# DSA outputs scaled by transposed reciprocals, scores of a job in neighbouring PSUM banks, one bank for outputs

## The chip, the cores and the metric

The kernel runs on one core of a Trainium2 chip. The metric is the device time of one execution in microseconds. Engines are named as in the profile: PE (TensorE; PEld is its weight load), DVE (VectorE), ACT (ScalarE), POOL (GpSimd), SP (SyncE, which issues the DMAs).

## The reference

One layer of a decoder on 1024 tokens with 16 meta tokens in front, width 1024, all float32. The input is RMS-normalised and projected; two attentions of 8 heads of 64 channels run side by side, stick-breaking attention (SB) and sparse attention chosen by an indexer (DSA). Their outputs are gated, merged, projected and followed by a squared-ReLU MLP. The part that the change touches is DSA for a block of 128 queries:

```python
logits = jnp.einsum('bqhd,bqkhd->bhqk', qb, kg) * (D_HEAD ** -0.5)   # kg: the 256 selected keys
logits = jnp.where(sel_ok[:, None], logits, -jnp.inf)
p = jax.nn.softmax(logits, axis=-1)
return jnp.einsum('bhqk,bqkhd->bqhd', p, vg)
```

The kernel does not gather: it computes all causal scores and adds a mask (`sel`, 0 or -1e30) for the keys that are not selected. The softmax divides by the row sum of the exponents.

## The kernel before, in words

Matrix products are made of float32 parts rounded to the PE's format: x = hi + lo, and a product is hi*hi + hi*lo + lo*hi, three matmuls. A stage of projections comes first (line 606), then 64 SB jobs, between which the rest of the projections is filled in, then 64 DSA jobs, then the branch stage (o_hi and o_lo times the branch weights, gates), the output projection and the MLP.

A job is one head and one block of 128 queries; block i has KEYS[i] = 16 + 128(i+1) keys, 144 to 1040. Each head takes its blocks in the order 7, 0, 6, 1, 5, 2, 4, 3 (`BLOCKS`). `JOBS` has the 64 SB jobs and then the 64 DSA jobs; NJ = 128. Every engine runs the same loop over j and does in iteration j, in this order:

- PE: `scores(j)` (line 637: keys in chunks of at most 512 columns, even in size, two matmuls each, into PSUM banks 2 and 3 in turn); `turn(j-2)` (657: transposes the weights a_buf, up to four 128-key tiles in one bank, a "group", into a ring of banks 4, 5, 6 and in the DSA stage also 0); the next head's `values` when j % 8 = 4; `product(j-3)` (667: three matmuls a tile into the output bank, 7 or 1 in turn in the DSA stage).
- DVE: in the DSA stage the reciprocal of job j-1's sum (`normalise`, 1028); `logits(j)` (1010: one instruction a chunk adds the mask to the score and takes the running minimum of the negated sum; each is recorded as two instructions on line 1024); `rest_weights(j-2)` (1038: the lo part of the transposed weights, which also frees the bank); for the last 16 jobs `rest_output` (1052: the lo part of an output).
- ACT: `normalise(j-1)` (781, line 785: a_buf times the reciprocal, in place); `round_weights(j-2)` (786: the hi part); `exponent(j)` (773, line 778: exp with the row sum as by-product); `output(j-3)` (805: copies a product out of PSUM, to `o_pair` for the first 48 DSA jobs, and for the last 16, `PAIRED` and later, as hi part straight to `o_hi`). `round_pair` (821) casts a finished pair of heads (16 jobs) of `o_pair` to `o_hi` in iterations `PAIR_AT`; POOL takes the rest.
- SP: loads queries, keys and values of the next head (`load_head`) when the last scores of the head before are done.

An instruction waits for semaphores (`wait_ge`) that others count up; `turn_bank` (620) waits for the bank's last group to be freed, `product` for the last output of its bank. The queue of an engine is in order.

Of the kernel before, what the change touches and what calls it, by code (L numbers as in the profile page):

```python
# [20 lines left out]
P = 128  # L21
# [84 lines left out]
NZ_SB = Z_END[NJ // 2 - 1]  # L106
TPN, TP_BANK = {}, []
# [21 lines left out]
def o_bank(j):  # L129

    return 7 if j < NJ // 2 or j % 2 == 0 else 1
# [49 lines left out]
RELOAD = [STEPS + 6 + 10 * p_ for p_ in range(4)]  # L181
PAIR_AT = [STEPS + 16 * (p_ + 1) + 3 for p_ in range(3)]
PAIRED = STEPS + 48
# [22 lines left out]
def build(nc, x, meta, w_units, b_gate, g_pre, g_post, g_mlp_pre, g_mlp_post, ident, strict, fill,  # L206
          rope_i, rope_d, out):
    with ExitStack() as ctx:
# [203 lines left out]
        o_pair = at("o_pair", [P, 3, SEQ], F32, O_SC)  # L412
# [20 lines left out]
        with ExitStack() as st:  # L433
            bk = [psum(st, f"bk{i}", [P, HALF]) for i in range(8)]
            pj = bk[0:2]
            pj_done, hi_evac, lo_evac = sem("f_pj"), sem("f_hi"), sem("f_lo")
# [10 lines left out]
            pv_done, o_free, oh_done = sem("f_pv"), sem("f_ofree"), sem("f_oh")  # L447
            o_spilled = [sem("f_ospill0"), sem("f_ospill1")]
            or_in, or_hi, or_lo = [sem("f_orin0"), sem("f_orin1")], sem("f_orhi"), sem("f_orlo")
            op_hi, op_lo, mask_done = sem("f_ophi"), sem("f_oplo"), sem("f_mask")  # L450
            block = st.enter_context(nc.Block())

            @block.sync
            def _(sp):
# [44 lines left out]
                def load_head(g):  # L499
                    s = g % 2  # L500
                    if g >= 2:
                        sp.wait_ge(z_ready, Z_END[8 * (g - 1) - 1])
# [64 lines left out]
            def _(pool):  # L567
# [8 lines left out]
                for j in range(NJ // 2 + 1, NJ + 6):  # L576
# [4 lines left out]
                    for p in range(3):  # L581
                        if j == PAIR_AT[p]:
                            pool.wait_ge(op_hi, p + 1)
                            pool.tensor_tensor(o_lo[:, 4 + p, :], o_pair[:, p, :], o_hi[:, 4 + p, :].bitcast(F32), ALU.subtract).then_inc(op_lo, 1)

            @block.tensor
            def _(pe):
# [32 lines left out]
                def turn_bank(n):  # L620
                    if TP_PREV[n] is not None:
                        pe.wait_ge(tp_free, TP_PREV[n] + 1)
                    elif TP_BANK[n] < 2:
                        bank_read(NC_ALL - 2 + (TP_BANK[n] + NC_ALL) % 2)
# [12 lines left out]
                def scores(j):  # L637
# [5 lines left out]
                    for m, (c0, c1) in enumerate(ZCH[i]):  # L643
                        z = Z_END[j] - len(ZCH[i]) + m
                        if 2 <= z < NZ_SB + 2:
                            pe.wait_ge(zs_used, z - 1)
                        elif z >= 2:
                            pe.wait_ge(zd_used, z - 1 - NZ_SB)
                        dst = bk[2 + z % 2][:, 0:c1 - c0]
# [5 lines left out]
                        mm.then_inc(z_ready, 1)  # L655

                def turn(j):
                    t, g, i = JOBS[j]
                    pe.wait_ge(a_done, j + 1)
# [6 lines left out]

                def product(j):
                    t, g, i = JOBS[j]
                    if j == NJ // 2 + 1:
                        bank_read(NC_ALL - 2 + (1 + NC_ALL) % 2)  # L670
                    elif j > NJ // 2 + 1:
                        pe.wait_ge(o_free, j - 1)
                    elif j:
                        pe.wait_ge(o_free, j)
                    tiles = [x_ for g_ in groups(i) for x_ in g_]
                    for m, (c, r) in enumerate(tiles):
                        if m % 4 == 0:
                            pe.wait_ge(tp_free, TPN["p", j, m // 4] + 1)
                        for k, (v, w) in enumerate(((v_hi, pt_hi), (v_hi, pt_lo), (v_lo, pt_hi))):
                            mm = pe.matmul(bk[o_bank(j)][0:DH, 0:P], v[0:r, g % 2, c, :], w[0:r, j % 2, c, :], start=m == 0 and k == 0,  # L680
# [19 lines left out]
                for j in range(NJ + 3):  # L700
# [6 lines left out]
                    if j % NB == 4 and j // NB + 1 < 2 * H:  # L707
                        values(j // NB + 1)
                    for n, kt in FILL[j][1]:
# [10 lines left out]
            def _(act):  # L720
# [84 lines left out]
                def output(j):  # L805
                    t, g, i = JOBS[j]
                    act.wait_ge(pv_done, j + 1)
                    if t == SB:
                        if j >= 2:
                            act.wait_ge(o_spilled[j % 2], 16 * (j // 2))  # L810
                        act.copy(o_st[:, j % 2], bk[o_bank(j)][0:DH, 0:P]).then_inc(o_free, 1)
                    elif j < PAIRED:
                        r = DH * (g % 2)
                        if j == NJ // 2:
                            act.wait_ge(mask_done, 1)
                        act.copy(o_pair[r:r + DH, g // 2 - 4, i * P:(i + 1) * P], bk[o_bank(j)][0:DH, 0:P]).then_inc(o_free, 1)
                    else:
                        r = DH * (g % 2)
                        act.copy(o_hi[r:r + DH, g // 2, i * P:(i + 1) * P], bk[o_bank(j)][0:DH, 0:P]).then_inc(oh_done, 1)

                def round_pair(p):
                    act.wait_ge(o_free, STEPS + 16 * (p + 1))
                    act.copy(o_hi[:, 4 + p, :], o_pair[:, p, :]).then_inc(op_hi, 1)
# [11 lines left out]
                for j in range(NJ + 3):  # L835
# [6 lines left out]
                    if 1 <= j < NJ + 1 and JOBS[j - 1][0] == DS:  # L842
                        normalise(j - 1)
# [18 lines left out]
            def _(dve):  # L862
# [147 lines left out]
                def logits(j):  # L1010
                    t, g, i = JOBS[j]
                    s, keys = j % 2, KEYS[i]
                    last = 3e38
# [4 lines left out]
                    for m, (c0, c1) in enumerate(ZCH[i]):  # L1018
                        z = Z_END[j] - len(ZCH[i]) + m
                        dve.wait_ge(z_ready, z + 1)  # L1020
                        if m:
                            dve.wait_ge(zd_used, z - NZ_SB)
                        out = small[:, 16 + s:17 + s] if c1 == keys else small[:, 18 + m:19 + m]
                        dve.tensor_tensor_reduce(n_buf[:, s, c0:c1], bk[2 + z % 2][:, 0:c1 - c0], sel[:, BOFF[i] + c0:BOFF[i] + c1],
# [3 lines left out]
                def normalise(j):  # L1028
                    t, g, i = JOBS[j]
                    s, e, keys = j % 2, j - NJ // 2, KEYS[i]  # L1030
                    dve.wait_ge(exp_done, e + 1)
                    if e >= 2:
                        dve.wait_ge(a_done, j - 1)
                    dve.reciprocal(small[:, 24 + s:25 + s], small[:, 20 + j % 4:21 + j % 4]).then_inc(recip, 1)

                def rest_weights(j):
                    t, g, i = JOBS[j]
                    for k, tiles in enumerate(groups(i)):
                        n, m = TPN["p", j, k], len(tiles)
                        dve.wait_ge(tp_hi, n + 1)  # L1040
# [4 lines left out]
                def rest_values(g):  # L1045
                    for half in range(2):
                        n = TPN["v", g, half]
                        dve.wait_ge(tp_hi, n + 1)
                        dst, src = value_parts(g, half, n)
                        dve.tensor_tensor(v_lo[dst], src, v_hi[dst].bitcast(F32), ALU.subtract).then_inc(tp_free, 1)  # L1050

                def rest_output(j):
                    t, g, i = JOBS[j]
                    r = DH * (g % 2)
                    dst = (slice(r, r + DH), g // 2, slice(i * P, (i + 1) * P))
                    dve.wait_ge(oh_done, j + 1 - PAIRED)
                    dve.tensor_tensor(o_lo[dst], bk[o_bank(j)][0:DH, 0:P], o_hi[dst].bitcast(F32), ALU.subtract).then_inc(o_free, 1)  # L1057
# [18 lines left out]
                for j in range(NJ + 4):  # L1076
                    if 1 <= j < NJ + 1:
                        if JOBS[j - 1][0] == SB:
                            stick(j - 1)
                        else:  # L1080
                            normalise(j - 1)
# [10 lines left out]
                    if j - 4 >= PAIRED:  # L1092
                        rest_output(j - 4)
# [458 lines left out]
```

## Time and profile before

| | |
|---|---|
| median of 3 runs | 1851.16 us (1847.76 to 1852.23) |
| the profiled execution | 1850.96 us |
| its span, first to last instruction | 1849.2 us |
| PE busy | 1763.0 us (95%) |
| DVE busy | 1022.0 us (55%) |
| ACT busy | 703.3 us (38%) |
| POOL busy | 398.4 us (22%) |
| DSA stage | about 744 to 947 us of the span |

Busy times are sums over an engine's instructions without overlap. An idle stretch is put down to the instruction whose end released the engine.

### The profile page before, as it was taken

Reading aid. Unit: us, or ns where it says so; the run is one execution under the profiler, and the core shown is the slowest. Engines: PE = TensorE matmul, PEld = TensorE weight load, DVE = VectorE, ACT = ScalarE, POOL = GpSimd, SP = SyncE. Lnnn points to the kernel's source line nnn. Section 1 sums busy time; section 2 is a strip of 40 time slices with the busy share of each in tenths; the row PEclk is TensorE's granted clock in tenths of the full one; section 3 lists DMA queues with packets and bytes.
Section 4 is the critical chain, followed back from the end, with each engine's and each line's share of the span. In section 5 each row is a group of like instructions: output and inputs, shape, how many; then the busy total and the mean of one; then the engine's idle time right before and its main releaser. Section 6 shows DMA issues by size and latency. Waiting matters only on the chain. (4 is left out here: it accounts for less than half of the span.)

```text
span 1849.2 us, 25696 instructions
## 1 busy us (share of the span) xinstructions
PE 1763.0 (95%) x10056; PEld 1497.1 (81%) x10056; DVE 1022.0 (55%) x1764; ACT 703.3 (38%) x1375; POOL 398.4 (22%) x174
## 2 busy tenths in 40 slices
PE   3999999999999999899999899999999999999998
PEld 3989888899878878788878688888888888888886
DVE  5277788999999997576744244322222222222225
ACT  5256444444444444699941232302121121203032
POOL 1112222221111111111014510404041222314033
PEclk6999999999999999899999899999999999999999
DMA  4565424424323423444124432202020211112023
GB/s 133 172 187 147 134 74 131 140 85 111 112 68 96 114 67 102 104 95 100 42 103 139 169 114 91 91 12 80 12 80 22 70 41 51 51 41 71 21 75 142
DMA packets 65584, 170.55 MB, mean 92 GB/s; under 512 B 9320, under 2 KB 23976, under 8 KB 65464
## 3 DMA queue, kind: packets, MB, share of 16 engines
q1 hardware_dynamic: 65464, 168.91, 30.3%
q8 instruction: 80, 1.31, 0.3%
q14 instruction: 40, 0.33, 0.1%
HBM read 126.47 MB, written 42.41 MB: 91 GB/s over the span
## 5 line engine op out<-in xcount | busy, mean ns | idle before, releaser
L606 PE MATMUL bk<-x_hi,w_hi 128*128 128x512 f32 (+2 forms) x832 | 308.6, 371 | 6.3 <-PEq L284 6.3
L606 PE MATMUL bk<-x_lo,w_hi 128*128 128x512 f32 (+2 forms) x832 | 298.2, 358 | 0.0
L606 PE MATMUL bk<-x_hi,w_lo 128*128 128x512 f32 (+2 forms) x832 | 297.6, 358 | 0.0
L265 POOL TENSOR_TENSOR w_lo<-w_raw,w_hi 128x1024 fp32r<-128x1024 f32 x53 | 131.3, 2479 | 483.9 <-ACT w_hi L261 483.8
L1382 ACT ACTIVATE relu<-bank 128x1024 f32<-128x1024 f32 x32 | 32.9, 1029 | 504.7 <-PE bank L1293 504.7
L1293 PE MATMUL bank<-m_hi,w_hi 128*128 128x512 f32 x512 | 199.5, 390 | 0.0
L1293 PE MATMUL bank<-m_hi,w_lo 128*128 128x512 f32 x512 | 199.2, 389 | 0.0
L1293 PE MATMUL bank<-m_lo,w_hi 128*128 128x512 f32 x512 | 199.2, 389 | 0.0
L947 DVE TENSOR_SCALAR_CACHE_REDUCE sel<-sc,st_bits 128x272 bf16<-128x272 f32 (+6 forms) x217 | 184.2, 890 | 0.9
L606 PEld LDWEIGHTS bk<-x_hi,w_hi 128*128 128x128 f32 x832 | 158.7, 191 | 22.1 <-POOL w_lo L265 6.4
L1463 DVE TENSOR_TENSOR acc<-acc,bank 128x1024 f32<-128x1024 f32 x56 | 68.3, 1220 | 192.6 <-PE bank L1269 191.7
L606 PEld LDWEIGHTS bk<-x_hi,w_lo 128*128 128x128 f32 x832 | 157.7, 189 | 17.4
L1257 POOL TENSOR_TENSOR w_lo<-w_raw,w_hi 128x1024 fp32r<-128x1024 f32 x32 | 82.9, 2596 | 403.1 <-ACT w_hi L1358 403.1
L606 PEld LDWEIGHTS bk<-x_lo,w_hi 128*128 128x128 f32 x832 | 158.1, 190 | 13.3
L1042 DVE TENSOR_TENSOR pt_lo<-bk,pt_hi 128x512 fp32r<-128x512 f32 (+2 forms) x224 | 120.1, 571 | 85.5 <-ACT pt_hi L794 85.0
L1450 DVE TENSOR_TENSOR sq<-relu 128x1024 f32<-128x1024 f32 x32 | 39.2, 1225 | 227.9 <-ACT relu L1382 227.9
L680 PE MATMUL bk<-pt_hi,v_hi 128*64 128x128 f32 (+1 forms) x704 | 151.0, 241 | 6.0 <-DVE o_lo L1057 3.2
L794 ACT CAST pt_hi<-bk 128x512 fp32r<-128x512 f32 (+2 forms) x224 | 100.6, 495 | 110.2 <-PE bk L664 110.2
L680 PE MATMUL bk<-pt_lo,v_hi 128*64 128x128 f32 (+1 forms) x704 | 140.0, 225 | 0.0
L680 PE MATMUL bk<-pt_hi,v_lo 128*64 128x128 f32 (+1 forms) x704 | 139.6, 225 | 0.0
L680 PEld LDWEIGHTS bk<-pt_hi,v_hi 128*64 128x64 f32 (+1 forms) x704 | 96.3, 137 | 23.7 <-DVE o_lo L1057 5.6
L1293 PEld LDWEIGHTS bank<-m_hi,w_lo 128*128 128x128 f32 x512 | 96.1, 188 | 20.0
(177 smaller groups left out, 3586.1 us busy)
## 6 DMA issues: line engine op xcount, KB each, us to landing
w_raw<-w_units SPq DMA_DIRECT2D x99, 512.0 KB, 3.7
raw<-w_units SPq DMA_DIRECT2D x24, 512.0 KB, 3.5
k_hi<-k_d SPq DMA_DIRECT2D x32, 260.0 KB, 5.3
k_lo<-k_d SPq DMA_DIRECT2D x32, 260.0 KB, 5.9
q_st<-q_d SPq DMA_DIRECT2D x32, 256.0 KB, 4.7
g_d<-stage_hi SPq DMA_DIRECT2D x32, 256.0 KB
gate<-g_d SPq DMA_DIRECT2D x16, 512.0 KB, 4.4
v_raw<-v_d SPq DMA_DIRECT2D x16, 260.0 KB, 7.2
```

The source lines that it names most:

```text
L265: pool.tensor_tensor(w_lo[:, s], w_raw[:, s], w_hi[:, s].bitcast(F32), ALU.subtract).then_inc(lo_done, 1)
L606: mm = pe.matmul(pj[b][:, 0:c1 - c0], w[:, s, kt, :], a[:, kt, c0:c1], start=kt == 0 and k == 0, stop=kt == KT - 1 and k == 2)
L680: mm = pe.matmul(bk[o_bank(j)][0:DH, 0:P], v[0:r, g % 2, c, :], w[0:r, j % 2, c, :], start=m == 0 and k == 0, stop=m == len(tiles) - 1 and ...
L794: act.copy(pt_hi[:, j % 2, 4 * k:4 * k + m, :], bk[TP_BANK[n]][:, 0:m * P].rearrange("p (c k) -> p c k", c=m)).then_inc(tp_hi, 1)
L947: op(dve.tensor_scalar(sel[:, BOFF[b]:BOFF[b] + KEYS[b]], sc[:, blk(b)], cand[:, j:j + 1], None, ALU.is_ge, ALU.add, accum_out=cnt[:, j:j ...
L1042: dve.tensor_tensor(pt_lo[dst], bk[TP_BANK[n]][:, 0:m * P].rearrange("p (c k) -> p c k", c=m), pt_hi[dst].bitcast(F32), ALU.subtract).then ...
L1257: pool.tensor_tensor(unit_lo(v), raw_ring[(v - V0) % 3], unit_hi(v).bitcast(F32), ALU.subtract).then_inc(lo_done, 1)
L1293: mm = pe.matmul(m1_ps[n][:, c * HALF:(c + 1) * HALF], w[s][:, kt, :], a[:, kt, c * HALF:(c + 1) * HALF], start=kt == 0 and i == 0, stop=k ...
L1382: act.activation(relu8[:], m1_ps[n][:], ACT.Relu).then_inc(relu_done, 1)
L1450: dve.tensor_tensor(sq[:], relu8[:], relu8[:], ALU.mult).then_inc(sq_done, 1)
L1463: dve.tensor_tensor(acc[:, t], acc[:, t], m2_ps[g][:], ALU.add).then_inc(acc_done, 1)
```

## The change

- The DSA weights are no longer scaled. ACT's `normalise` and DVE's one-column reciprocal are gone; `turn` waits for the exponent. The row sums of a pair of heads are collected in 16 columns of `small`, and after 16 jobs DVE makes 1024 columns of reciprocals in one instruction (`reciprocals`: each sum broadcast to 64 columns). PE transposes them in eight 128x128 pieces (`turn_sums`), so that they lie like the outputs, and DVE multiplies the pair's outputs by them (`scale_pair`). For the last pair the transposed reciprocals are only copied, and multiplication, rounding and rest are done at the start of the branch stage, whose first PE unit waits for them ahead of its last tile.
- Banks 0 to 3 become one PSUM tile `quad`. A job's score chunks lie in neighbouring banks (`DS_BANKS`), and one DVE instruction takes two of them; block 7 has three chunks and two instructions.
- The transposes have banks 4, 5, 6; the DSA outputs have bank 7 alone, and all go through `o_pair`. `rest_output` is gone.

The core of the diff (`...` marks what is left out):

```diff
+PAIR_AT = [NJ // 2 + 16 * (p_ + 1) + 3 for p_ in range(3)] + [NJ + 1]
-    ring = (4, 5, 6) if j < NJ // 2 + 2 else (4, 5, 6, 0)
+    ring = (4, 5, 6)
-    return 7 if j < NJ // 2 or j % 2 == 0 else 1
+O_BANK = 7
+DS_BANKS = {7: (0, 1, 2), 0: (3,), 6: (0, 1), 1: (2,), 5: (0, 1), 2: (2,), 4: (0, 1), 3: (2, 3)}
...
+        o_pair = [at(f"o_pair{p}", [P, SEQ], F32, O_SC + 4096 * p if p < 3 else O_STAGE) for p in range(4)]
+        r_wide = at("r_wide", [P, SEQ], F32, O_SC + 3 * 4096)
+        r_last = at("r_last", [P, SEQ], F32, O_STAGE + 4096)
...
 def scores(j):
+                        b = 2 + z % 2 if t == SB else DS_BANKS[i][m]
+                        elif BANK_BUSY[j, m] is not None:
+                            pe.wait_ge(zd_used, BANK_BUSY[j, m] + 1)
...
 def turn(j):
-                    pe.wait_ge(a_done, j + 1)
+                    if t == SB:
+                        pe.wait_ge(a_done, j + 1)
+                    else:
+                        pe.wait_ge(exp_done, j + 1 - NJ // 2)
...
+                def turn_sums(p):
+                    pe.wait_ge(recip, p + 1)
+                    for half in range(2):
+                        n = TPN["r", p, half]
+                        turn_bank(n)
+                        for m in range(4):
+                            i = 4 * half + m
+                            mm = pe.transpose(bk[TP_BANK[n]][:, m * P:(m + 1) * P], r_wide[:, i * P:(i + 1) * P], idf[:])
+                        mm.then_inc(tp_ready, 1)
 def product(j):
-                    elif j > NJ // 2 + 1:
-                        pe.wait_ge(o_free, j - 1)
-                    elif j:
+                    if j:
                         pe.wait_ge(o_free, j)
...
 ACT
-                def normalise(j):
-                    keys, s = KEYS[JOBS[j][2]], j % 2
-                    a = a_buf[:, j % 3, 0:keys]
-                    act.wait_ge(recip, j - NJ // 2 + 1)
-                    act.activation(a, a, ACT.Copy, scale=small[:, 24 + s:25 + s]).then_inc(a_done, 1)
+                        act.copy(o_pair[p][r:r + DH, i * P:(i + 1) * P], bk[O_BANK][0:DH, 0:P]).then_inc(o_free, 1)
                 def round_pair(p):
-                    act.wait_ge(o_free, STEPS + 16 * (p + 1))
+                    act.wait_ge(tp_free, TPN["r", p, 1] + 1)
...
 DVE, logits(j)
+                    for m0, m1, n in LOGIT_OPS[j]:
+                        c0, c1, b = ZCH[i][m0][0], ZCH[i][m1 - 1][1], DS_BANKS[i][m0]
+                        w = (c1 - c0) // (m1 - m0)
+                        dve.wait_ge(ds_ready, n + 1)
...
+                        dve.tensor_tensor_reduce(n_buf[:, s, c0:c1].rearrange("p (b w) -> p b w", w=w), quad[:, b:b + m1 - m0, 0:w],
+                                                 sel[:, BOFF[i] + c0:BOFF[i] + c1].rearrange("p (b w) -> p b w", w=w),
                                                  -DH ** -0.5, last, ALU.add, ALU.min, out).then_inc(zd_used, 1)
...
+                def reciprocals(p):
+                    dve.wait_ge(exp_done, 16 * (p + 1))
+                    sums = small[:, 128 + 16 * p:144 + 16 * p]
+                    if p:
+                        dve.wait_ge(tp_ready, TPN["r", p - 1, 1] + 1)
+                    dve.reciprocal(r_wide[:].rearrange("p (c d) -> p c d", d=DH), sums.unsqueeze(2).broadcast_to([P, 16, DH])).then_inc(recip, 1)
+                def scale_pair(p):
+                    if p < 3:
+                        dve.wait_ge(o_free, NJ // 2 + 16 * (p + 1))
+                    else:
+                        dve.wait_ge(or_lo, 4)
+                    for half in range(2):
...
+                        if p < 3:
+                            dve.tensor_tensor(o_pair[p][:, cols], o_pair[p][:, cols], src, ALU.mult).then_inc(tp_free, 1)
+                        else:
+                            dve.tensor_copy(r_last[:, cols], src).then_inc(tp_free, 1)
-                def rest_output(j):
...
 for j in range(NJ + 4), DVE
+                    if j > NJ // 2 and j % 16 == 0:
+                        reciprocals((j - NJ // 2) // 16 - 1)
                     if j < NJ and JOBS[j][0] == DS:
                         logits(j)
...
 the branch stage
+                                     before=lambda kt: pe.wait_ge(last_lo, 1) if k == 0 and kt == KT - 1 else None)
+                act.wait_ge(last_mul, 1)
+                act.copy(o_hi[:, KT - 1, :], o_pair[3][:]).then_inc(last_hi, 1)
+                dve.tensor_tensor(o_pair[3][:], o_pair[3][:], r_last[:], ALU.mult).then_inc(last_mul, 1)
+                dve.wait_ge(last_hi, 1)
+                dve.tensor_tensor(o_lo[:, KT - 1, :], o_pair[3][:], o_hi[:, KT - 1, :].bitcast(F32), ALU.subtract).then_inc(last_lo, 1)
```

## Rows read from the trace of the kernel before

**Rows 1.** The page's busy table: busy us, share of the span, instructions.
```profile
PE 1763.0 (95%) x10056; PEld 1497.1 (81%) x10056; DVE 1022.0 (55%) x1764; ACT 703.3 (38%) x1375; POOL 398.4 (22%) x174
```
**Rows 2.** Busy PE, PEld, DVE, ACT, POOL by stretch; granted clock, DMA share, GB/s.
```profile
748.46:780.46 32.00, 24.24 (x204) 21.38 (x205) 16.06 (x51) 20.42 (x49) 0.00 (x0) 0.84 0.44 103
780.46:918.92 138.46, 130.48 (x1279) 113.25 (x1280) 98.67 (x317) 128.36 (x297) 16.71 (x7) 0.99 0.39 88
918.92:947.48 28.56, 24.81 (x239) 21.18 (x240) 18.57 (x60) 21.43 (x52) 0.00 (x0) 0.94 0.01 1
```
**Rows 3.** Waits of PEld in 780.46 to 918.92: total, times, longest.
```profile
PEld bk L651 <- DVE small L1024: 8.0, 9, 2.0
...
PEld bk L680 <- DVE o_lo L1057: 1.1, 2, 0.6
...
PEld bk L664 <- DVE pt_lo L1042: 0.3, 1, 0.3
```
**Rows 4.** Groups by line in 755 to 944: busy, mean ns | idle before, releasers.
```profile
L785 ACT ACTIVATE a_buf<-a_buf,small 128x912 f32<-128x912 f32 (+7 forms) x62 | 49.0, 791 | 5.9 <-DVE small L1034 3.4
L680 PEld LDWEIGHTS bk<-pt_hi,v_hi 128*64 128x64 f32 (+1 forms) x349 | 48.1, 138 | 14.9 <-DVE o_lo L1057 5.6 <-issue 2.7 <-ACT o_st L811 0.2
```
**Rows 5.** Timeline around block 7's turn (PEld, ACT): start, us, instruction.
```profile
877.58 1.06 PEld L664 LDWEIGHTS bk<-idf,a_buf 128*128 128x128 f32 x9
880.37 0.14 PEld L680 LDWEIGHTS bk<-pt_hi,v_hi 128*64 128x64 f32 x1
880.59 0.25 ACT L816 COPY o_pair<-bk 64x128 f32<-64x128 f32 x1
```
**Rows 6.** Timeline of the branch stage, PEld.
```profile
948.28 0.42 PEld L275 LDWEIGHTS br<-o_hi,w_lo 128*128 128x128 f32 x2
948.74 0.42 PEld L275 LDWEIGHTS br<-o_hi,w_hi 128*128 128x128 f32 x2
```
**Rows 7.** Tile small, DVE: ns min/median/max, first and last start, forms.
```profile
L1034 DVE RECIPROCAL small<-small x64: 140/164/165, 749.7 to 939.7; 128x1 f32<-128x1 f32 x64
L1421 DVE TENSOR_SCALAR small<-small x8: 146/147/154, 1067.8 to 1142.6; 128x1 f32<-128x1 f32 x8
...
L1443 DVE SCALAR_TENSOR_TENSOR nn<-hh,small,gb x8: 1284/1285/1286, 1073.8 to 1147.8; 128x1024 f32<-128x1024 f32 x8
L1466 DVE TENSOR_SCALAR small<-small x8: 153/154/155, 1808.6 to 1842.9; 128x1 f32<-128x1 f32 x8
```
**Rows 8.** Timeline of a head boundary, DVE and PEld.
```profile
846.18 0.19 PEld L651 LDWEIGHTS bk<-k_hi,q_st 128*128 128x128 f32 x1
...
846.47 0.69 DVE L1042 TENSOR_TENSOR pt_lo<-bk,pt_hi 128x512 fp32r<-128x512 f32 x1 [0.42 <-ACT pt_hi L794]
...
847.20 0.16 DVE L1034 RECIPROCAL small<-small 128x1 f32<-128x1 f32 x1
847.32 0.52 DVE L1024 CUSTOM_DVE_ANT_0 n_buf<-bk,sel 128x348 f32<-128x348 f32 x1
...
847.90 0.19 PEld L651 LDWEIGHTS bk<-k_hi,q_st 128*128 128x128 f32 x1 [1.10 <-DVE small L1024]
...
849.23 0.08 DVE L1024 DVE_READ_ACCUMULATOR2_ANT small<- 128x1 f32 x1
...
850.17 0.48 PEld L664 LDWEIGHTS bk<-idf,a_buf 128*128 128x128 f32 x5
```
**Rows 9.** The wait for the second DSA head's values, then stretches behind it.
```profile
766.18 0.94 PEld L634 LDWEIGHTS bk<-idf,v_raw 64*128 64x128 f32 x9 [6.13 <-DMA v_raw<-v_d]
...
766.00:772.00 6.00, 5.82 (x41) 5.19 (x41) 2.28 (x7) 3.74 (x9) 0.00 (x0) 0.50 0.01 3
772.00:780.00 8.00, 7.54 (x72) 6.67 (x71) 5.73 (x19) 5.94 (x14) 0.00 (x0) 0.99 0.37 85
```
**Rows 10.** Timeline of the last exponent's sum and block 4's rest.
```profile
939.21 0.19 ACT L778 ACTIVATION_READ_ACCUMULATOR a_buf<-n_buf,small 128x1 f32 x1
...
941.17 1.02 DVE L1042 TENSOR_TENSOR pt_lo<-bk,pt_hi 128x512 fp32r<-128x512 f32 x2 [1.27 <-ACT pt_hi L794]
```

More of the change, by code:

```diff
@@ L106 @@
 NZ_SB = Z_END[NJ // 2 - 1]
+RELOAD = [NJ // 2 + 6 + 10 * p_ for p_ in range(4)]
+PAIR_AT = [NJ // 2 + 16 * (p_ + 1) + 3 for p_ in range(3)] + [NJ + 1]
 TPN, TP_BANK = {}, []
 def tp_take(key, j):
-    ring = (4, 5, 6) if j < NJ // 2 + 2 else (4, 5, 6, 0)
+    ring = (4, 5, 6)
     TPN[key] = len(TP_BANK)
@@ L125 @@
             tp_take(("v", j_ // NB + 1, half_), j_)
-TP_PREV = [max([m_ for m_ in range(n_) if TP_BANK[m_] == b_], default=None) for n_, b_ in enumerate(TP_BANK)]
-def o_bank(j):
-    return 7 if j < NJ // 2 or j % 2 == 0 else 1
+    if j_ in PAIR_AT:
+        for half_ in range(2):
+            tp_take(("r", PAIR_AT.index(j_), half_), j_)
+R_GROUPS = sorted(n_ for key_, n_ in TPN.items() if key_[0] == "r")
+HI_NO = [n_ - sum(r_ < n_ for r_ in R_GROUPS) for n_ in range(len(TP_BANK))]
+TP_PREV = [max([m_ for m_ in range(n_) if TP_BANK[m_] == b_], default=None) for n_, b_ in enumerate(TP_BANK)]
+O_BANK = 7
+DS_BANKS = {7: (0, 1, 2), 0: (3,), 6: (0, 1), 1: (2,), 5: (0, 1), 2: (2,), 4: (0, 1), 3: (2, 3)}
+LOGIT_OPS, CHUNK_OP, BANK_BUSY = {}, {}, {}
+last_op_ = {}
+for j_ in range(NJ // 2, NJ):
+    n_ = len(ZCH[JOBS[j_][2]])
+    LOGIT_OPS[j_] = []
+    for m0_, m1_ in ([(0, 2), (2, 3)] if n_ == 3 else [(0, n_)]):
+        LOGIT_OPS[j_].append((m0_, m1_, sum(len(x_) for x_ in LOGIT_OPS.values())))
+    for m0_, m1_, op_ in LOGIT_OPS[j_]:
+        for m_ in range(m0_, m1_):
+            b_ = DS_BANKS[JOBS[j_][2]][m_]
+            CHUNK_OP[j_, m_] = m_ == m1_ - 1
+            BANK_BUSY[j_, m_] = last_op_.get(b_)
+            last_op_[b_] = op_
 W_AT = FIRST_CHUNK[3] + 1
@@ L433, in build @@
         with ExitStack() as st:
-            bk = [psum(st, f"bk{i}", [P, HALF]) for i in range(8)]
+            quad = psum(st, "quad", [P, 4, HALF])
+            bk = [quad[:, i] for i in range(4)] + [psum(st, f"bk{i}", [P, HALF]) for i in range(4, 8)]
             pj = bk[0:2]
+            ds_ready = sem("f_dsready")
             pj_done, hi_evac, lo_evac = sem("f_pj"), sem("f_hi"), sem("f_lo")
@@ L583, in _ @@
                             pool.wait_ge(op_hi, p + 1)
-                            pool.tensor_tensor(o_lo[:, 4 + p, :], o_pair[:, p, :], o_hi[:, 4 + p, :].bitcast(F32), ALU.subtract).then_inc(op_lo, 1)
+                            pool.tensor_tensor(o_lo[:, 4 + p, :], o_pair[p][:], o_hi[:, 4 + p, :].bitcast(F32), ALU.subtract).then_inc(op_lo, 1)
             @block.tensor
@@ L679, in product @@
                         for k, (v, w) in enumerate(((v_hi, pt_hi), (v_hi, pt_lo), (v_lo, pt_hi))):
-                            mm = pe.matmul(bk[o_bank(j)][0:DH, 0:P], v[0:r, g % 2, c, :], w[0:r, j % 2, c, :], start=m == 0 and k == 0,
+                            mm = pe.matmul(bk[O_BANK][0:DH, 0:P], v[0:r, g % 2, c, :], w[0:r, j % 2, c, :], start=m == 0 and k == 0,
                                            stop=m == len(tiles) - 1 and k == 2)
@@ L1017, in logits @@
                         dve.wait_ge(exp_done, j - 1 - NJ // 2)
[L1018 to L1024, printed above, removed]
+                    last = 3e38
@@ L1047, in rest_values @@
                         n = TPN["v", g, half]
-                        dve.wait_ge(tp_hi, n + 1)
+                        dve.wait_ge(tp_hi, HI_NO[n] + 1)
                         dst, src = value_parts(g, half, n)
                         dve.tensor_tensor(v_lo[dst], src, v_hi[dst].bitcast(F32), ALU.subtract).then_inc(tp_free, 1)
-                def rest_output(j):
[L1053 to L1057, printed above, removed]
                 for n in range(NC_STEP):
@@ L1076, in _ @@
                 for j in range(NJ + 4):
[L1077 to L1081, printed above, removed]
+                    if 1 <= j < NJ + 1 and JOBS[j - 1][0] == SB:
+                        stick(j - 1)
+                    if j > NJ // 2 and j % 16 == 0:
+                        reciprocals((j - NJ // 2) // 16 - 1)
                     if j < NJ and JOBS[j][0] == DS:
```

81 lines of the change are left out of this document (41 added, 40 removed).

## The prediction, made before the changed kernel was run

> **What bounds the kernel now.** I read the page's busy table first: over the whole span PE is 95% busy, the other engines little over half or less [rows 1]. That mixes stages. The change touches only the DSA stage, so I cut it by the exponent of block 7, which opens every head: a first stretch of 32.0 us, six even heads of 138.46 us (23.08 us each), and a last stretch of 28.56 us up to the first matmul of the branch stage, 199 us in all [rows 2]. In the six even heads ACT is busy 128.36 us of 138.46 (93%) and PE 130.48 us (94%): two engines near their limit. A busy PE here is not a full one, since pipelined matmuls overlap, so I read what its weight-load side waited for: 15.1 us of idle over the six heads (the sum of seven rows), 2.5 us a head, of which 8.0 us for a score bank that DVE had not read [rows 3]. The work of PE without waits is therefore 23.08 - 2.5 = 20.6 us a head. That is the floor for this stage: the change leaves all of PE's score, transpose and product matmuls in place.
>
> **What is removed.** ACT loses 64 scalings of the weights, 0.79 us each in the mean, plus the idle in front of them [rows 4]. 128.36/6 - 8 x 0.79 = 15.1 us of ACT work a head are left, far under 20.6, so ACT no longer sets the pace and what I can gain is PE's idle, 2.5 us a head at most. DVE loses 64 one-column reciprocals and, with 9 score operations a head for 14, some five fixed costs; it is not the bound (98.67 us busy of 138.46 [rows 2]), so I cost that at nothing, covered by PE's 20.6 us. The wait for a score bank goes: each bank is now reused two jobs later, except bank 2 of block 7, whose reader is one job back and done by then.
>
> **What comes in its place on PE.** The outputs have one bank where they had two, so a product waits for ACT's copy of the product just before, and that copy stands behind ACT's rounding and exponent. Where a small job follows a large one PE gets there first. In the steady head shown it turned block 7's nine tiles at 877.58 and began its product at 880.37; the copy of the output before began only at 880.59 and took 0.25 us [rows 5]. With one bank that is a wait of 0.5 us. The same pattern stands behind block 5 (values and a short product); the others have a product of 1.4 us or more in between. I take two waits, 1.1 us a head. Three banks for transposes instead of four I cost at nothing: the bank wanted is three groups back, and its DVE rest is done within an iteration; if that cover goes (below) it matters. Steady gain: 2.5 - 1.1 = 1.4 us a head, x8 = -11 us. In the last two heads products also waited for DVE's o_lo; 5.6 us in the stage, 1.1 of it in the six even heads [rows 3, 4]. That instruction goes, and I take -2.5 us for it, since part comes back as the wait on ACT.
>
> **Turned reciprocals on PE.** Eight 128-row transposes a pair; nine took 1.06 us [rows 5], so 0.94 us x3 = +2.8 us on the path. The fourth eight lie in the tail, inside the wait below. The two multiplies a pair cost DVE 2 x 0.69 us, the length of its 512-column rest [rows 8]; the cast is the old one; the 40 us that DVE has idle in the six heads cover both. The last pair's multiply, cast and subtraction at the start of the branch stage are three instructions of 1024 columns, 1.3 us each by the row of that size [rows 7], 3.9 us in all; PE asks for them after 42 matmuls that come in pairs every 0.46 us [rows 6], 9.7 us, so they are hidden and I count nothing.
>
> **The wide reciprocal: the term that decides.** Four times DVE computes 128x1024 reciprocals in one instruction. The trace has the operation at one column only: 164 ns, beside medians of 147 to 154 ns for a one-column TENSOR_SCALAR [rows 7]. If the difference is a fixed cost, 1024 columns take what a 1024-column operation takes, 1.3 us [rows 7]. If it is the price of a column, the smallest difference between single values, 164 against 155 ns, gives 9 us, and the difference of the medians at line 1421, 17 ns, gives 17 us. Nearest to the operation are its own rows, and in every pairing in the trace it is slower than a simple operation on the same tile; I take 9 us and keep 1.3 and 17 as ends. No row of this case shows it.
>
> What 9 us cost: three of them stand at a head boundary, where the one-column reciprocal starts at 847.20 [rows 8], in front of the block-7 logits and the rests of the weights. At that point PE has begun the scores (846.18); it goes on through two jobs until it turns the second group of block 3, which needs the transpose bank that DVE must empty behind it. On PE's side that is 3.4 us after the start of the scores: the segments between 846.18 and 850.17, less the 1.1 us of bank wait that goes, and half of the next turn [rows 8]. On DVE's side it is 0.1 (exponent ready), 9, 1.8 (the logits, 2.0 us from 847.32 to 849.31 now, less one fixed cost), 0.7 (first rest): 11.6 us [rows 8]. PE stands still for 8.2 us. Then its clock: after the 6.13 us wait for v_raw the granted clock was 0.50 for the next 6 us, the lower level of 1.2 GHz, and back at 0.99 after that [rows 9]; 6 us at half speed lose 3 us of work. With about 0.7 us of that absorbed in waits that would be there anyway: 10.5 us each, x3 = +31.5 us. The fourth waits for the last exponent, whose sum is read at 939.21, so DVE is free at 948.5; the rest of block 4 began at 941.17 and is pushed to that time [rows 10]. That is 7.3 us, and the turned sums behind it delay the last two products by 0.7: +8 us.
>
> **Sum**: -11 - 2.5 + 2.8 + 31.5 + 8 = +28.8 us. The profiled execution took 1850.96 us (span 1849.2), almost the median 1851.16, so 1880 us. About 0.3%, 5.6 us, is what a measurement of this kernel can tell from no change.
>
> **Rivals.** (1) *The wide reciprocal is cheap* (1.3 us): it fits in DVE's slack, which is 40 us over six heads, and the kernel ends faster: -11 - 2.5 + 2.8 + 1 = -10, 1841 us. For it: a 10 ns difference may be a longer way through the pipeline. Against it: the difference is there in all pairs. The Trainium skill, in Vector Engine (DVE) Microarchitecture Reference, Anatomy of a single slice, lets the divide chain span all eight slices, which could be read as one result a cycle; that would be this rival's time. The point from which it decides: four times the excess over what DVE has spare pays back the 11 us at about 3.6 us an instruction, 3.5 ns a column. Chance 0.14. (2) *In between*, 2.5 to 7 us: 1846 to 1865 us. Chance 0.06. (3) *One output bank takes all the gain*: with cheap reciprocals PE waits for ACT's copy in most jobs as it waited for scores; the 11 us come back on rival 1's time, 1852 us. Chance 0.04. (4) *The column costs 17 ns*: 8 us more, four times, 1912 us. Chance 0.04. That the change does not do what it says I leave out: the scaling, its wait and the second bank are gone from the code. My forecast has 0.72. Its own range is 1862 to 1893: steady gain from 0 to 2.5 us a head (+11 or -9), the stop between 8.5 and 12 us each.
>
> **How the numbers follow.** The forecast's own range leaves some 0.04 of its 0.72 outside; to hold 8 in 10 the range has to take in the in-between case, the one-bank case and the slow edge of the cheap case, so 1842 to 1893. Faster by over 0.3%: rival 1 and an edge of 2, 0.15. Within 0.3%: rival 3 and an edge of 2, 0.05. Slower: 0.80.
>
> **What would show it.** In the changed trace: RECIPROCAL r_wide x4 with a mean near 9 us; DVE solid for those stretches; PE idle of some 8 us near the starts of the third, fifth and seventh DSA head, its clock at 0.5 behind each; between them heads of about 21.7 us with ACT at some 70%; no wait of the scores on DVE but waits of the products on ACT's o_pair; the branch stage starting some 29 us later. A r_wide row near 1.3 us makes the forecast wrong at its root and rival 1 right; heads still at 23 us would break the steady gain; a stop with the clock staying high would cut 3 us from each.

## The result and the profile after

The changed kernel takes **1882.9 us** in the median of four runs (1880.9 to 1883.86), the kernel before 1849.57 us (four runs): a ratio of 1.017, 95% interval 1.015 to 1.0189, so slower. The profiled execution took 1882.88 us, with a span of 1881.1 us; that is 31.9 us more span than before. The forecast of 1880 us was near by luck: it will turn out that one group of its terms was 11 us too high and the other 14 us too low.

The page's busy table, which answers to [rows 1]. ACT lost 39 us of work and PE gained 12 us; nothing in this table says "32 us slower":
```profile
PE 1774.9 (94%) x10088; PEld 1507.7 (80%) x10088; DVE 1035.2 (55%) x1618; ACT 664.3 (35%) x1312; POOL 399.5 (21%) x174
```
Busy PE, PEld, DVE, ACT and POOL by stretch, cut as in [rows 2], then granted clock, DMA share, GB/s; the last two lines are the stretch behind the second stop (below) and one where no stop is near:
```profile
748.90:780.33 31.43, 23.52 (x207) 20.77 (x207) 13.30 (x31) 14.88 (x41) 0.00 (x0) 0.84 0.44 103
780.33:945.49 165.16, 141.03 (x1304) 122.51 (x1303) 109.27 (x214) 98.04 (x247) 16.69 (x7) 0.92 0.33 74
945.49:977.85 32.36, 25.40 (x245) 21.89 (x244) 21.66 (x35) 15.99 (x43) 0.00 (x0) 0.95 0.00 1
866.00:871.40 5.40, 4.02 (x23) 3.35 (x24) 2.18 (x8) 2.94 (x8) 0.00 (x0) 0.50 0.40 103
847.00:853.00 6.00, 5.08 (x34) 4.47 (x35) 1.44 (x5) 3.00 (x8) 2.38 (x1) 0.62 0.00 0
```
The time is in the six even heads: 165.16 us where it was 138.46 (+26.7), and in the last stretch (+3.8); the first is 0.6 us shorter, and 2.0 us lie outside the stage (0.4 ahead of it and 1.5 behind). ACT is busy for 59% of the six heads (93% before), PE for 85%, and the granted clock is 0.92 where it was 0.99.

What PE's weight-load side waited for in those six heads (total us, times, longest), which answers to [rows 3]. L701 turns the weights, L723 is the product, L659 turns the values:
```profile
PEld bk L701 <- DVE pt_lo L1093: 15.7, 3, 5.4
PEld bk L723 <- ACT o_pair L857: 12.0, 18, 1.7
PEld bk L659 <- DVE pt_lo L1093: 2.8, 6, 0.5
PEld bk L659 <- issue: 1.3, 6, 0.2
```
The score waits of before (8.0 us) are gone. In their place stand three long stops for a transpose bank, 18 waits for ACT's copy out of the one output bank, and six short waits of the values for one of three transpose banks.

The tile r_wide (min, median and max ns of one; first and last start; form) prices what no row of before had:
```profile
L1071 DVE RECIPROCAL r_wide<-small x4: 6552/6552/6553, 801.2 to 964.6; 128x1024 f32<-128x1024 f32 x4
```
The timeline of the second of the three stops (start, length, engine, instruction, idle in front and who ended it), then of the last reciprocal and the start of the branch stage:
```profile
858.11 6.55 DVE L1071 RECIPROCAL r_wide<-small 128x1024 f32<-128x1024 f32 x1
...
860.96 0.42 PEld L701 LDWEIGHTS bk<-idf,a_buf 128*128 128x128 f32 x4
...
864.58 0.82 DVE L1061 CUSTOM_DVE_ANT_0 n_buf<-quad,sel 128x696 f32<-128x696 f32 x1
...
865.55 0.58 DVE L1061 CUSTOM_DVE_ANT_0 n_buf<-quad,sel,small 128x344 f32<-128x344 f32 x1
...
866.05 1.02 DVE L1093 TENSOR_TENSOR pt_lo<-bk,pt_hi 128x512 fp32r<-128x512 f32 x2
...
866.79 0.09 PEld L701 LDWEIGHTS bk<-idf,a_buf 128*16 128x16 f32 x1 [5.41 <-DVE pt_lo L1093]
...
964.63 6.55 DVE L1071 RECIPROCAL r_wide<-small 128x1024 f32<-128x1024 f32 x1
...
971.10 1.75 DVE L1093 TENSOR_TENSOR pt_lo<-bk,pt_hi 128x512 fp32r<-128x512 f32 x4
...
971.78 0.09 PEld L701 LDWEIGHTS bk<-idf,a_buf 128*16 128x16 f32 x1 [4.87 <-DVE pt_lo L1093]
...
977.85 0.30 PEld L291 LDWEIGHTS br<-o_hi,w_hi 128*128 128x128 f32 x2 [0.72 <-issue]
...
977.88 1.23 DVE L1213 TENSOR_TENSOR o_pair<-o_pair,r_last 128x1024 f32<-128x1024 f32 x1 [3.01 <-PEq L451]
...
980.22 1.23 DVE L1215 TENSOR_TENSOR o_lo<-o_pair,o_hi 128x1024 fp32r<-128x1024 f32 x1 [1.11 <-ACT o_hi L1203]
```
Read the first part downwards on DVE: reciprocal, logits, rests. PE turns four tiles at 860.96 and then has nothing that it may do until the rest at 866.05 has emptied a transpose bank: it stands for 5.41 us (5.15 us at the first stop, at 809.85). No instruction behind it on PE is late by itself; all of it is DVE's queue. The last pair's work at the branch stage (977.88 to 981.45) runs beside the matmuls, as said; PE has no wait for it.

### The profile page after: what moved, and what is told of

It reads as the page before. It is cut to its first block and busy times, and to the rows that moved or that the text cites. A ratio compares the mean times of both kernels' runs of the same rounds, so it can differ in the third digit from the quotient of the medians.

```text
span 1881.1 us, 25461 instructions
## 1 busy us (share of the span) xinstructions
PE 1774.9 (94%) x10088; PEld 1507.7 (80%) x10088; DVE 1035.2 (55%) x1618; ACT 664.3 (35%) x1312; POOL 399.5 (21%) x174
## 5 line engine op out<-in xcount | busy, mean ns | idle before, releaser
L633 PE MATMUL quad<-x_hi,w_hi 128*128 128x512 f32 (+2 forms) x832 | 308.8, 371 | 6.3 <-PEq L300 6.3
L633 PE MATMUL quad<-x_lo,w_hi 128*128 128x512 f32 (+2 forms) x832 | 298.4, 359 | 0.0
L633 PE MATMUL quad<-x_hi,w_lo 128*128 128x512 f32 (+2 forms) x832 | 297.8, 358 | 0.0
L633 PEld LDWEIGHTS quad<-x_hi,w_hi 128*128 128x128 f32 x832 | 158.9, 191 | 22.2 <-POOL w_lo L281 6.4
L633 PEld LDWEIGHTS quad<-x_hi,w_lo 128*128 128x128 f32 x832 | 157.8, 190 | 17.4
L633 PEld LDWEIGHTS quad<-x_lo,w_hi 128*128 128x128 f32 x832 | 158.3, 190 | 13.3
L723 PE MATMUL bk<-pt_hi,v_hi 128*64 128x128 f32 (+1 forms) x704 | 153.0, 243 | 10.8 <-ACT o_pair L857 8.8
L723 PE MATMUL bk<-pt_lo,v_hi 128*64 128x128 f32 (+1 forms) x704 | 141.9, 227 | 0.0
L723 PE MATMUL bk<-pt_hi,v_lo 128*64 128x128 f32 (+1 forms) x704 | 141.6, 227 | 0.0
L723 PEld LDWEIGHTS bk<-pt_hi,v_hi 128*64 128x64 f32 (+1 forms) x704 | 97.6, 139 | 30.8 <-ACT o_pair L857 15.2
L701 PE MATMUL bk<-idf,a_buf 128*128 128x128 f32 (+1 forms) x704 | 101.0, 277 | 19.6 <-DVE pt_lo L1093 19.6
```

What stands on the lines that cost most here:

```text
L633: mm = pe.matmul(pj[b][:, 0:c1 - c0], w[:, s, kt, :], a[:, kt, c0:c1], start=kt == 0 and k == 0, stop=kt == KT - 1 and k == 2)
L701: mm = pe.transpose(bk[TP_BANK[n]][0:r, m * P:(m + 1) * P], a_buf[:, j % 3, c * P:c * P + r], idf[:])
L723: mm = pe.matmul(bk[O_BANK][0:DH, 0:P], v[0:r, g % 2, c, :], w[0:r, j % 2, c, :], start=m == 0 and k == 0, stop=m == len(tiles) - 1 and k ...
```

## The experiments

Differences are taken against the median of the kernel before in the same batch (1850.87 us for e1 to e4, 1850.92 for e5 to e8, 1851.42 for e9 to e11). By that count the changed kernel stands at +33.3 us.

**e1: the reciprocals taken on 16 columns, then copied out wide.** Against the changed kernel:
```diff
-                    dve.reciprocal(r_wide[:].rearrange(...), sums.unsqueeze(2).broadcast_to([P, 16, DH])).then_inc(recip, 1)
+                    r16 = small[:, 192 + 16 * p:208 + 16 * p]
+                    dve.reciprocal(r16, sums).then_inc(r_small, 1)
+                    dve.wait_ge(r_small, p + 1)
+                    dve.tensor_copy(r_wide[:].rearrange(...), r16.unsqueeze(2).broadcast_to([P, 16, DH])).then_inc(recip, 1)
```

> The changed kernel, but DVE takes the reciprocals of a pair's 16 sums (16 columns) and copies them out to 1024 columns, instead of one 1024-column reciprocal of 6.55 us. Theory A (the four wide reciprocals stop PE some 5.3 us each and cost about 3 us of low clock behind, and that is the whole loss; the stage between them has gained nothing): 1883 - 3 x 8.3 - 5 = about 1853 us. Rival B (my prediction's steady gain of 1.4 us a head is there once the stops are gone): about 1842 us. Rival C (the loss has mostly another cause, one output bank or three transpose banks): no better than 1870 us.

Measured: 1855.24 us, ratio 1.0022 (1.0012 to 1.0032), +4.4 us. Its profile, first the groups by line (busy, mean ns | idle before):
```profile
L1075 DVE COPY r_wide<-small 128x1024 f32<-128x1024 f32 x4 | 2.8, 694 | 0.1
...
L1073 DVE RECIPROCAL small<-small 128x16 f32<-128x16 f32 x4 | 1.0, 253 | 0.1
```
Then the six even heads, busy by engine:
```profile
780.89:922.53 141.64, 132.23 (x1304) 114.75 (x1303) 92.50 (x217) 97.73 (x247) 16.69 (x7) 1.00 0.38 86
```
And what PEld waited for in them:
```profile
PEld bk L724 <- ACT o_pair L858: 12.2, 19, 1.7
PEld bk L660 <- DVE pt_lo L1097: 2.8, 6, 0.5
PEld bk L660 <- issue: 1.3, 6, 0.2
```
The stops are gone, the clock is 1.00, and 28.2 us of span (1881.1 - 1852.9) with them. Yet the kernel is not faster than before, and a head takes 141.64/6 = 23.6 us where 23.1 stood: theory A holds, and the forecast's steady gain is refuted (heads still at 23 us were its own sign for that). Where a wait for the output copy comes from stands in the timeline of the same run:
```profile
828.35 1.16 ACT L824 ACTIVATE a_buf<-n_buf,small 128x1040 f32<-128x1040 f32 x1 [0.16 <-DVE small L1062]
...
829.51 0.24 ACT L858 COPY o_pair<-bk 64x128 f32<-64x128 f32 x1
...
829.80 0.13 PEld L724 LDWEIGHTS bk<-pt_hi,v_hi 128*64 128x64 f32 x1 [0.75 <-ACT o_pair L858]
829.80 0.27 PE L724 MATMUL bk<-pt_hi,v_hi 128*64 128x128 f32 x1 [0.50 <-ACT o_pair L858]
```
The copy stands in ACT's queue behind the exponent of a large block; PE, now ahead, waits for both. (The matmul side of PE stood for 0.50 us where its weight-load side stood for 0.75, so the sums of PEld's waits are somewhat more than PE loses.)

**e2: the wide reciprocal alone, in the kernel before.** Nothing else of the change is in it:
```diff
+                    if j > NJ // 2 and j % 16 == 0:
+                        dve.wait_ge(exp_done, j - NJ // 2)
+                        dve.reciprocal(r_wide[:], small[:, 23:24].broadcast_to([P, SEQ])).then_inc(wide_done, 1)
```

> The kernel before, with one 1024-column reciprocal added on DVE ahead of the logits after every 16 DSA jobs (4 in all); its result is not used. Theory A: the instruction alone costs what the change lost, 3 x 8.3 + 5 = +30 us, about 1880 us. Rival (the cost depends on the change's three transpose banks and single output bank; four banks let PE run on for longer): +20 us or less, 1870 us.

Measured: 1885.56 us, ratio 1.019 (1.0173 to 1.0207), +34.7 us. The longest of PEld's waits in its six even heads, by releaser:
```profile
PEld bk L653 <- DVE small L1026: 26.9, 8, 7.6
```
One of the stops in the timeline:
```profile
857.05 6.53 DVE L1086 RECIPROCAL r_wide<-small 128x1024 f32<-128x1024 f32 x1
...
864.02 0.29 PEld L653 LDWEIGHTS bk<-k_hi,q_st 128*128 128x128 f32 x1 [7.65 <-DVE small L1026]
```
The instruction alone makes the kernel as slow as the whole change does. That the two totals agree is in part chance: in the changed kernel the same instruction is worth 33.3 - 4.4 = 28.9 us, and the other 4.4 are what e1 has left. PE stops sooner here, for a score bank, at 864.02 - 7.65 = 856.37, even before the instruction has begun; the changed kernel's new score banks let it run on until 866.79 - 5.41 = 861.38.

**e3: the same columns of reciprocals, in eight pieces of 128 behind the logits of eight jobs.**
```diff
-                    dve.reciprocal(r_wide[:].rearrange(...), sums.unsqueeze(2).broadcast_to([P, 16, DH])).then_inc(recip, 1)
+                    dve.reciprocal(r_wide[:, i * P:(i + 1) * P].rearrange(...), sums.unsqueeze(2).broadcast_to([P, 2, DH])).then_inc(recip, 1)
...
-                    if j > NJ // 2 and j % 16 == 0:
-                        reciprocals((j - NJ // 2) // 16 - 1)
                     if j < NJ and JOBS[j][0] == DS:
                         logits(j)
+                    if NJ // 2 < j <= NJ and JOBS[j - 1][1] % 2 == 1:
+                        reciprocals(j - 1)
```

> The changed kernel with the same reciprocals, but cut in eight pieces of 128 columns (about 0.87 us each, 7.0 us a pair), each behind the logits of the job that follows its sum. Theory A (what costs is that 6.55 us stand ahead of the logits in DVE's queue, not the work itself): equal to e1_cheap within 4 us, about 1855 us. Rival (DVE's work as such costs): between, some 1865 us or more.

Measured: 1857.12 us, ratio 1.0033 (1.0024 to 1.0043), +6.3 us. Its tile r_wide:
```profile
L1073 DVE RECIPROCAL r_wide<-small x32: 939/948/955, 780.9 to 946.8; 128x128 f32<-128x128 f32 x32
```
32 x 0.95 = 30.3 us of DVE work, more than the 26.2 us of the four wide ones, costs 2 us over e1, which the noise barely tells from nothing. So it was never the amount of work, but 6.55 us in one piece ahead of what PE needs next.

**e4: e1 with ACT's output copy ahead of the exponent.**
```diff
+                    if j >= 3 and JOBS[j - 3][0] == DS:
+                        output(j - 3)
                     if j < NJ and JOBS[j][0] == DS:
...
-                    if j >= 3:
+                    if j >= 3 and JOBS[j - 3][0] == SB:
                         output(j - 3)
```

> e1_cheap with ACT copying the output of job j-3 ahead of the exponent of job j instead of behind it. Theory (with one output bank PE waits for that copy: 9.0 us of PEld's idle over 112 us of the changed kernel's stage): it gives back up to 1.5 us a head, 8 to 12 us less than e1_cheap. Rival (ACT now waits for the product ahead of the exponent, and the exponent comes late): no gain, or some us slower than e1_cheap.

Measured: 1843.2 us, ratio 0.9962 (0.9949 to 0.9974), -7.7 us; 12.0 under e1. The waits of PEld in its six even heads:
```profile
PEld bk L702 <- DVE pt_lo L1099: 3.9, 4, 1.5
PEld bk L660 <- DVE pt_lo L1099: 3.8, 6, 1.0
```
The wait on o_pair is gone from the list, and the time went with it. This shows that the copy's place in the queue was the cost; part of it came back as waits for the three transpose banks (7.7 us in these two rows, 3.2 in e1).

**e5: e1 with one DVE instruction for each score chunk, as before.**
```diff
-    for m0_, m1_ in ([(0, 2), (2, 3)] if n_ == 3 else [(0, n_)]):
+    for m0_, m1_ in [(x_, x_ + 1) for x_ in range(n_)]:
```

> e1_cheap with one DVE instruction for each score chunk, as before the change, in the changed kernel's banks (14 instructions a head for 9). Theory (DVE has 49 us idle over the six even heads of e1_cheap, so the merging of instructions is hidden): within 3 us of e1_cheap, about 1855 us. Rival (the fixed costs saved lie on the path to the exponent): 5 us or more slower than e1_cheap.

Measured: 1855.06 us, ratio 1.0019 (1.0009 to 1.0029), +4.1 us, as e1. Merging mask and minimum over neighbouring banks is worth nothing measurable here.

**e6: e1's scaled outputs with the banks of before** (scores in two banks, a ring of four for transposes, two for outputs, one instruction per chunk). The diff against e5, cut to the bank choices:
```diff
-    ring = (4, 5, 6)
+    ring = (4, 5, 6) if j < NJ // 2 + 2 else (4, 5, 6, 0)
...
-O_BANK = 7
+def o_bank(j):
+    return 7 if j < NJ // 2 or j % 2 == 0 else 1
...
-                        dst = bk[b][:, 0:c1 - c0]
+                        dst = bk[2 + z % 2][:, 0:c1 - c0]
```

> e1_cheap (outputs scaled, cheap reciprocals) with the banks and score instructions of the kernel before: scores in two banks in turn, four banks for transposes, two for outputs. Theory (the new banks gave PE's score wait of 1.3 us a head away and took 2.0 us a head of wait for the output copy in its place): 12 us of output waits go and some 8 us of score waits come, 2 to 6 us faster than e1_cheap, 1850 us. Rival 1 (without the scaling on ACT both waits are gone): 1843 us or less. Rival 2 (the new banks were the better ones): slower than e1_cheap.

Measured: **1840.18 us**, ratio 0.9941 (0.9925 to 0.9958), -10.7 us: faster than both kernels. The six even heads, busy by engine:
```profile
781.80:913.69 131.89, 128.24 (x1303) 115.33 (x1304) 98.25 (x277) 96.46 (x248) 16.72 (x7) 1.00 0.41 92
```
What PEld waited for in them (L680 is a score, L663 turns the values, and quad is the tile that banks 0 to 3 belong to):
```profile
PEld quad L680 <- DVE small L1059: 5.4, 6, 1.1
PEld bk L663 <- issue: 0.7, 3, 0.2
PEld quad L663 <- issue: 0.7, 3, 0.2
```
My theory had the score waits of before come back in full and missed by 10 us; they are 5.4 us, not 8.0, and nothing waits for an output. The 3.2 us of waits for transpose banks in e1 are gone too, which the theory had left out. The first rival's time was right, but only one of its two waits is gone. The new banks cost 14.9 us (1855.06 - 1840.18), 9.8 of it in the six heads (141.64 in e1, 131.89 here).

**e7: e6 with the output copy first.** The same edit as e4's, on e6:
```diff
+                    if j >= 3 and JOBS[j - 3][0] == DS:
+                        output(j - 3)
```

> e6_old_banks with ACT copying output j-3 ahead of exponent j. Theory (copying first helps only by the single output bank): equal to e6_old_banks within 3 us. Rival (it helps by itself): 5 us or more faster.

Measured: 1846.81 us, ratio 0.9975 (0.9965 to 0.9986), 6.6 us slower than e6 where I expected no change. Waits of PEld in its six even heads:
```profile
PEld quad L680 <- DVE small L1061: 8.4, 6, 2.1
```
And the longest of ACT's waits there, in the same columns (this row has 5.8 us in 8 waits in e6):
```profile
ACT o_pair L856 <- PE bk L722: 15.6, 17, 1.6
```
With two banks the copy is not urgent. Put first, it makes ACT wait for PE's product before it may begin the exponent (outputs in bank 1 have a row of their own, 4.0 us in 13 waits, none in e6), and PE's wait for a score bank, 5.4 us in e6, grows to 8.4; how the one leads to the other I did not follow further.

**e8: the changed kernel with the output copy first**, wide reciprocals kept, by the same edit:
```diff
+                    if j >= 3 and JOBS[j - 3][0] == DS:
+                        output(j - 3)
```

> The changed kernel with its wide reciprocals, and ACT copying output j-3 ahead of exponent j. Theory (the stop behind the wide reciprocal and the wait for the output copy are two independent terms): 12 us less than the changed kernel, as e4_cheap_out_first was 12 us less than e1_cheap: 1871 us. Rival (they overlap): 1876 us or more.

Measured: 1874.44 us, ratio 1.0122 (1.0105 to 1.0139), +23.5 us: 9.8 us under the changed kernel by the distances to before, 12.0 in the pair with cheap reciprocals. Waits of PEld, 780 to 940 us:
```profile
PEld bk L701 <- DVE pt_lo L1095: 20.1, 4, 6.6
```
The longest stop grew from 5.4 to 6.6 us. The timeline shows why:
```profile
854.12 6.55 DVE L1073 RECIPROCAL r_wide<-small 128x1024 f32<-128x1024 f32 x1 [1.23 <-ACT a_buf L823]
...
862.80 0.09 PEld L701 LDWEIGHTS bk<-idf,a_buf 128*16 128x16 f32 x1 [6.61 <-DVE pt_lo L1095]
```
The reciprocal waits 1.23 us for the last exponent, which now stands behind the copy (in the changed kernel it waits for nothing), so PE stops 2.07 us after it has begun (862.80 - 6.61 - 854.12) instead of 3.27 us. The two costs are not quite additive; the result lies between theory and rival.

**e9: e6 with one output bank.**
```diff
-    return 7 if j < NJ // 2 or j % 2 == 0 else 1
+    return 7
```
With it a product waits again for the copy of the output just before.

> e6_old_banks with one output bank instead of two. Theory (of the 15 us between e1_cheap and e6_old_banks nearly all is PE's wait for the copy of the output before, 12.2 us over six heads of e1_cheap): +12 us, about 1852 us. Rival (most of the 15 us is the ring of three transpose banks): +4 us or less, 1844 us.

Measured: 1856.12 us, ratio 1.0025 (1.0012 to 1.0038), +4.7 us, so 15.4 us over e6. Waits of PEld, 780 to 915 us:
```profile
PEld bk L718 <- ACT o_pair L852: 13.2, 20, 1.6
```
**e10: e6 with three transpose banks.**
```diff
-    ring = (4, 5, 6) if j < NJ // 2 + 2 else (4, 5, 6, 0)
+    ring = (4, 5, 6)
```

> e6_old_banks with three transpose banks (4, 5, 6) instead of four. Theory (only the second values group of a head has to wait, 0.5 us): +3 to +4 us, about 1844 us. Rival (three banks are the main loss): +10 us or more.

Measured: 1845.08 us, ratio 0.9968 (0.9958 to 0.9977), -6.3 us, so 4.4 us over e6. Waits of PEld, 781 to 915 us:
```profile
PEld bk L663 <- DVE pt_lo L1093: 3.4, 6, 0.8
```
Each edit has its own new wait, and each wait accounts for most of its time. Together they would give 19.8 us, the step from e6 to e5 is 14.9: the bank layout of the change gives some back by its four score banks, or one wait covers the other. The 5.4 us of score waits in e6 that e1's list does not have are about the difference, which is for the first; no run takes the two apart.

**e11: e6 without reciprocals, turned sums and scaling.** The DSA outputs are then not divided by their sums; the last pair is multiplied by itself, so that this multiply stays. The edit, cut to the calls:
```diff
-                    if j in PAIR_AT:
-                        turn_sums(PAIR_AT.index(j))
...
-                    if j > NJ // 2 and j % 16 == 0:
-                        reciprocals((j - NJ // 2) // 16 - 1)
...
-                    if j in PAIR_AT:
-                        scale_pair(PAIR_AT.index(j))
```

> e6_old_banks without reciprocals, turned sums and the scaling of the outputs: the DSA outputs are not divided by their sums, and the last pair is multiplied by itself in the place of that scaling. What the scaling of the outputs costs by my sum: 3 x 0.94 us on PE plus about 1 us for the fourth in the tail, so 4 us faster, about 1836 us. Rival (it is hidden): within 1.5 us of e6_old_banks.

Measured: 1835.7 us, ratio 0.9914 (0.9897 to 0.993), -15.7 us. The six even heads:
```profile
782.01:910.09 128.08, 125.61 (x1279) 112.66 (x1280) 92.09 (x265) 96.50 (x248) 16.69 (x7) 1.00 0.42 95
```
All that reciprocals, turned sums and the multiplies of three pairs still cost in e6 is 5.0 us. In the six heads it is 3.8 us (131.89 - 128.08), of which 2.6 are the busy time of PE's 24 transposes (128.24 - 125.61); PE's score waits, 5.4 us in e6, are 4.2 here.

## Why the time was right and its terms were not

The forecast had +28.8 us on the profiled execution, made of +39.5 for the four wide reciprocals and -10.7 for the rest. The spans give +31.9: +28.2 for the reciprocals (changed kernel less e1) and +3.7 for the rest (e1 less before). The first was 11.3 us too high, the second 14.4 too low. That 1880 stood so near 1882.9 is luck. By the conditions that the prediction set, its second rival came true: the instruction took between 2.5 and 7 us, and the stop with the clock behind it cost at most (15.3 + 8.2)/3 = 7.8 us (below), under the 8.5 from which the forecast's own range began. That rival's time, 1846 to 1865 us, is wrong even by the forecast's own working: four stops shorter by 2 us, at 7 us an instruction, make 1872, and with the 6.55 measured it is 1870. Most of the other 13 us are the gain that did not come.

**The wide reciprocal: the mechanism was right, the size off.** The mis-sized term is "I take 9 us": it measured 6.55. With 6.55 put into the prediction's own working the stop on PE is 8.2 - 2.45 = 5.75 us (measured 5.15 to 5.41) and the one in the tail 7.3 - 2.45 = 4.85 us (measured 4.87). Place, chain and order were as said, down to the group of tiles at which PE stops. The one-column row could not give the price: 9 ns came from 164 less 155 ns, of which a fixed part is unknown. The runs give 6.25 ns a column, (6552 - 253)/1008 from 16 columns and (6552 - 948)/896 from 128. The Trainium skill, in VectorE: DVE Perf Modes, First, the fixed hardware budget, gives the operation a repeat count of 8, from which I had estimated 8.5 us; measured are six cycles of the page's 0.96 GHz a column, not eight, and the measurement decides. The other reading, one result a cycle, from the Trainium skill's Vector Engine (DVE) Microarchitecture Reference, Anatomy of a single slice, is refuted by the same rows.

The rival that rested on the cheap price falls in two ways: the instruction is not cheap, and where it is made cheap (e1) the kernel is not faster.

**The low clock behind the stops was there.** The granted clock is 0.50 from 866.00 to 871.40, behind the second stop, the level of 1.2 GHz, as forecast. Its price over the six heads: 165.16 - 141.64 = 23.5 us, of which 15.3 are the stops (15.7 less e1's 0.4 at that line); 8.2 are left, where 3 x 3 was forecast. That includes a fourth low stretch near 850 us that has no stop ahead of it, so one stop costs less than 3 us of it.

**The steady gain did not come.** Before, the six heads took 138.46 us; the forecast without the stops had 138.46 - 6 x 1.4 + 2.8 = 132.9, and e1 has 141.64, 8.8 us more. Two steps failed. "I take two waits, 1.1 us a head": it was 12.2 us in six heads, three waits and 2.0 us a head, because I looked at one pattern, a small job behind a large one where ACT was late by a copy, in a trace in which ACT and PE were both near their limit (93 and 94%). Once ACT's scalings are gone, PE runs ahead, and the copy behind a large exponent is late at more jobs (0.75 us at 829.80). "Three banks I cost at nothing": 3.2 us in six heads of e1 (2.8 for the values, 0.4 for the weights), 4.4 us in e10. The forecast also took away waits without a releaser, of which 1.8 us stay; against these three stands 1.8 us less work of PE than reckoned.

The rest of the 14.4 us, from the spans of e1 and before, lies about half in the first and last stretches, 2.4 us shorter where 5.3 were forecast (8 x 1.4 is 11.2, less 8.4, and 2.5 for o_lo), and half outside the stage, 2.9 us, which no run explains and which single executions of this kernel can differ by.

The rival "one output bank takes all the gain" had a chance of 0.04; its mechanism is what e1 and e9 show, at 1855 us even a little more than it said, though with 19 waits in 48 jobs and not "in most jobs", and with the transpose banks adding to it.

**What was right.** PE's floor: e1's six heads less the 17.2 us of waits, with the two short ones that are not shown (0.5 and 0.4), are 124.4 us, 20.7 us a head, against 20.6 forecast before the turned sums and 21.0 with them. ACT is busy for 69% of the six heads of e1, against 70% forecast. The turned sums were put at 2.8 us, and e11 finds 2.6 us of PE's busy time for them. Merging the logits is worth nothing (e5), and the last pair is hidden (977.88). That the scaling of the weights held PE back shows in e6, with the banks of before: 138.46 - 131.89 = 6.6 us in six heads, turned sums included. The forecast had 5.6 there, but for other banks, so that the two are near proves nothing; and what e6 shows is the whole new scaling, not ACT's part of it alone.

## What to carry to other kernels

Before a bank is taken from a stage, ask of every engine that empties it what stands ahead of that work in its queue once the engines' lead has changed; the waits of the old trace are no guide, and the copy that gained 12 us at the head of its queue with one bank cost 7 us there with two. A long instruction in a queue that a bound engine depends on costs its length less the lead, and the low clock behind the stop: compute on the narrow operand and copy it wide (0.25 + 0.69 us for 6.55), or split it. When several terms of a sum are unknown, one run with a term removed tells more than a total that fits.

## What the runs showed of the hardware

DVE's RECIPROCAL of float32 takes 164, 253, 948 and 6552 ns for 1, 16, 128 and 1024 columns on 128 partitions, 6.25 ns a further column from 16 columns on, while a COPY of 1024 columns takes 694 ns and a multiply 1.23 us. The granted clock of the changed kernel was 0.62 from 847 to 853 us, where PE had waited only briefly:
```profile
846.04 0.09 PEld L659 LDWEIGHTS bk<-idf,v_raw 64*16 64x16 f32 x1 [0.46 <-DVE pt_lo L1093]
...
848.72 0.18 PEld L723 LDWEIGHTS bk<-pt_hi,v_hi 128*64 128x64 f32 x1 [1.21 <-ACT o_pair L857]
```
e1 has waits of the same kind (19 on o_pair, the longest 1.7 us) and shows 1.00 over all six heads. What let the clock fall there stays open.
